# Two transformer blocks on one core: the two weight rings are moved 112 bytes past a multiple of 128

## The reference, cut to what matters

```python
def reference(x, ...):          # x: (1, 512, 1024) float32
    x = first_block(x, ...)     # rmsnorm, a 1024 -> 1536 projection, gated causal conv of 31 taps,
                                # layernorm, pools, 1024 -> 1024; then swiglu 1024 -> 2816 -> 1024
    return second_block(x, ...) # two layers: attention, layernorm,
                                # conv_ffn 1024 -> 2 x 2816 -> 1024, layernorm
def swiglu(x, w_gate, w_up, w_down):
    return (silu(x @ w_gate) * (x @ w_up)) @ w_down
```

## The kernel before, in words

| tensor | start within 128, before | after | distance of the moving tensor from its weights, before | after |
|---|---|---|---|---|
| XH, XL, yout, last_rows, raw | 0 | 0 | X from W: 0 | 16 |
| WH, WL | 0 | 112 | | |
| par, ones, identr, masks, work, small | 0 | 0 | | |
| HH, HL | 64 | 32 | H from W: 64 | 48 |
| PTH, PTL, OH, OL, OF, pmap, VX, QX and the rest of the attention | 64 | 96 | O from W: 64 | 112 |
| dg_h, dg_l | 64 | 64 | | |
| u_h, u_l, group 0 and group 1 | 64 + 4m and 124 + 4m | the same | u from dg: 4m and 60 + 4m | the same |

## Time and profile before

### The profile page before, as it was taken

How to read it: one execution, slowest core, us unless ns; L and a number is a source line. 1 busy time by engine, 2 the same in 40 slices (tenths; PEclk the granted TensorE clock), 3 DMA queues, 4 the chain that set the end, 5 groups by cost and what they waited for, 6 DMA issues and landing times.

```text
span 1818.9 us, 26859 instructions
## 1 busy us (share of the span) xinstructions
PE 1774.2 (98%) x8755; PEld 1477.6 (81%) x8755; DVE 765.2 (42%) x1382; ACT 795.8 (44%) x1674; POOL 1029.9 (57%) x926
## 2 busy tenths in 40 slices
PE   8999999999999999999999999999999999999997
PEld 6879888888887888788888888877777888888886
DVE  7963000001235556553333322487875533333224
ACT  5644323322245555464444422555565644444231
POOL 7856555555462333466666655555554666666551
PEclk9999999999999999999999999999999999999999
DMA  5312333323334454323333233333332233332332
GB/s 153 92 47 82 104 92 92 101 87 103 91 90 115 123 133 122 86 73 99 102 92 94 85 104 87 82 94 81 87 77 79 63 111 93 96 100 78 104 91 97
DMA packets 327253, 171.94 MB, mean 95 GB/s; under 512 B 43459, under 2 KB 316949, under 8 KB 327189
## 3 DMA queue, kind: packets, MB, share of 16 engines
q1 hardware_dynamic: 327172, 171.12, 33.8%
q10 hardware_dynamic: 16, 0.00, 0.0%
HBM read 152.15 MB, written 2.10 MB: 85 GB/s over the span
## 4 chain that ended last, share of the span: by engine, by line
PE 87%; DVE 5%; POOL 3%; ACT 2%; issue 1%; DMA 1%; SPq 0%; DVEq 0%; ACTq 0%; POOLq 0%
PE bank L982 24%; PE bank L984 24%; PE bank L983 24%; PE attended L982 2%; PE attended L983 2%; PE attended L984 2%; PE turned L1423 1%; POOL WL L741 1%; PE attended L1439 1%; PE bank L1055 1%; PE bank L1067 1%; POOL psums L804 1%; PE bank L1068 1%; DVE small L2453 0%; PE score L1406 0%
## 5 line engine op out<-in xcount | busy, mean ns | idle before, releaser
L741 POOL TENSOR_TENSOR WL<-raw,WH 128x512 fp32r<-128x512 f32 (+3 forms) x656 | 774.8, 1203 | 555.6 <-ACT WH L1604 553.1
L982 PE MATMUL bank<-XL,WH 128*128 128x512 f32 x1432 | 568.8, 397 | 3.7 <-DVE work L2576 1.2
L984 PE MATMUL bank<-XH,WL 128*128 128x512 f32 x1432 | 557.8, 390 | 0.0
L983 PE MATMUL bank<-XH,WH 128*128 128x512 f32 x1432 | 557.4, 389 | 0.0
L1604 ACT ACTIVATE WH<-raw 128x512 fp32r<-128x512 f32 (+3 forms) x656 | 338.5, 565 | 307.7 <-PE bank L984 190.9
L984 PEld LDWEIGHTS bank<-XH,WL 128*128 128x128 f32 x1432 | 269.7, 188 | 56.8
L982 PEld LDWEIGHTS bank<-XL,WH 128*128 128x128 f32 x1432 | 270.1, 189 | 55.6 <-DVE work L2576 1.5
L983 PEld LDWEIGHTS bank<-XH,WH 128*128 128x128 f32 x1432 | 270.4, 189 | 49.9
L982 PE MATMUL bank<-HL,WH 128*128 128x512 f32 (+1 forms) x528 | 200.6, 380 | 0.0
L983 PE MATMUL bank<-HH,WH 128*128 128x512 f32 (+1 forms) x528 | 200.3, 379 | 0.0
L984 PE MATMUL bank<-HH,WL 128*128 128x512 f32 (+1 forms) x528 | 200.3, 379 | 0.0
(11 more groups left out here) (366 smaller groups left out, 2532.0 us busy)
## 6 DMA issues: line engine op xcount, KB each, us to landing
raw<-in_ffn_w_in SPq DMA_DIRECT2D x88, 512.0 KB, 3.8
raw<-in_w_gate SPq DMA_DIRECT2D x22, 512.0 KB, 3.8
raw<-in_w_up SPq DMA_DIRECT2D x22, 512.0 KB, 3.9
raw<-in_ffn_w_out SPq DMA_DIRECT2D x28, 384.0 KB, 3.3
raw<-in_ffn_w_out SPq DMA_DIRECT2D x28, 320.0 KB, 3.2
raw<-in_a_w_in SPq DMA_DIRECT2D x16, 512.0 KB, 4.2
raw<-in_kv_w SPq DMA_DIRECT2D x32, 256.0 KB, 3.2
raw<-in_w_in SPq DMA_DIRECT2D x12, 512.0 KB, 3.8
```

What stands on the lines that cost most here:

```text
L741: pool.tensor_tensor(wl, x, wh, ALU.subtract).then_inc(w_lo, 1)
L982: pe.matmul(out_, wh, xl, start=start, stop=False)
L983: pe.matmul(out_, wh, xh, start=False, stop=False)
L984: return pe.matmul(out_, wl, xh, start=False, stop=stop)
```

## The change

The two rings get a room of their own and begin 16 bytes into it; three unused tensors (96, 96 and 32 bytes) move what follows. No instruction is added, removed or reordered; only addresses change. WH's room is 16384 + 128 bytes and WL's 16384 + 32, so that `par` and what follows it stay at multiples of 128.

```diff
-        WH = sb("WH", [P, SLOTS, DT, P], F32R)
-        WL = sb("WL", [P, SLOTS, DT, P], F32R)
+        sb("before_w", [P, 24])
+        WH = sb("WH", [P, SLOTS * DT * P + 32], F32R)[:, 4:4 + SLOTS * DT * P].rearrange("p (s k n) -> p s k n", s=SLOTS, k=DT)
+        WL = sb("WL", [P, SLOTS * DT * P + 8], F32R)[:, 4:4 + SLOTS * DT * P].rearrange("p (s k n) -> p s k n", s=SLOTS, k=DT)
...
         ffn = ExitStack()
+        sb("before_h", [P, 24], stack=ffn)
         HH = sb("HH", [P, FT, S], F32R, stack=ffn)
...
         att = ExitStack()
+        sb("before_o", [P, 8], stack=att)
         PTH = sb("PTH", [P, 2, QT * KEYS + S - P], F32R, stack=att)
```

## The result

Two runs of the changed kernel gave 1836.26 and 1841.02 us, median 1838.64, against 1817.22: a ratio of 1.0118, 95% interval 1.0087 to 1.0149. The change makes the kernel 21 us slower, where 22 us less had been forecast, and the time is outside the stated range. It lies near rival C (1844).

A forecast was written before the change was run, and what follows sets the result against it. It took PE's stream of matmuls, number times pitch, as the bound. Terms -8.9 - 1.0 - 11.9 + 1.7 - 2.5 + 0.8 = -21.8 us gave a median of 1795.4 us, range 1758 to 1824.

The forecast's parts named there:

- rival C: X's 512-column matmuls leave their best place, distance 0, and slow to 233.3 ns: +26.7 us, median 1844; chance 0.10.
- X from 0 to 16 bytes: X's matmuls against W each lose 2 ns: -8.9 us for 4440 of 512 columns, -1.0 us for 480 of 256.
- the forecast of 118: Pitch in ns forecast for 256-column matmuls at the new distances, from the convolution's taps, against 120 at distance 0.
- H from 64 to 48: H's matmuls against W: 512 columns fall to 224.7 ns, 8.6 less, -11.9 us; 256 columns cost +1.7 us.
- O stayed: O's matmuls against W, moved from 64 to 112: 8.9 ns less at 512 columns, -2.5 us; 256 columns cost +0.8 us.
- the work of ACT and POOL on WH and WL with odd starts: Writing and reading weight rings off multiples of 32 bytes: costed at nothing, up to +4 us over the run.
- B: The new distances have the small surplus, 512 columns at 220.4 ns: -52.1 us in all, median 1765; chance 0.27.
- D: No change: pitches come from something the change leaves alone, such as slice lengths or address bits above 128 bytes; 1817; chance 0.13.

The follow-up runs named there:

- all0: Against the kernel before: H and the attention's tensors moved 64 bytes on, so X, H and O are all at distance 0 from the weights; 1809.95 us, ratio 0.9968.
- w128: Against the kernel before: the rings and everything behind them moved by 128 bytes, X unmoved; 1842.03 us, ratio 1.0123.
- near: The change's distances (X 16, H 48, O 112 bytes) held within 512 and alike for WH and WL; 1821.53 us, ratio 1.0020 against the kernel before.
- w64: Against the kernel before: the rings alone moved by 64 bytes, putting X at distance 64 and H and O at 0 within 128; 1834.33 us, ratio 1.0104.
- h0odd: Against the kernel before: both rings moved 16 bytes on, H at exactly 0 within 512 from them, X at 496; one run, 1829.01 us.
- w16: Against the kernel before: the rings alone moved by 16 bytes, so they start at 16 within 32; one run, 1839.12 us.
- x16: Rings at 112 as in the change, H kept 64 bytes from them within 128, O's start as before; 1835.88 us, ratio 1.0115 against the kernel before.
- wl64: Against the kernel before: WL's ring alone moved 64 bytes on, X at 0 from WH and 192 from WL; one run, 1828.39 us.
- xl64: Against the kernel before: XL moved 64 bytes on from XH, with 128 bytes ahead of raw that also moved the rings by 128; one run, 1831.8 us.
- abs64: Against the kernel before: everything moved by 64 bytes, all distances kept and all absolute starts new; 1815.61 us, ratio 0.9993.
- w256: Against the kernel before: the rings and everything behind them moved by 256 bytes, X unmoved; 1817.50 us, ratio 1.0003.

## Why the prediction was wrong, point by point

**The bound was right.** A stream of matmuls whose pitch is set by placement, and no wait: PE's share stayed at 98%, and the time goes with the pitches of X and H: from 1810 us with both at 226.7 ns (all0) to 1842 with both at 233.3 (w128).

**The step that failed** is "X from 0 to 16 bytes", which took 2 ns off X's 4440 matmuls of 512 columns; they gained 6.1 ns each, +27.1 us in place of -8.9. Two things were wrong in it. First, it carried a difference from 256 columns to 512 "as distance 0 has the same surplus at both lengths". At 256 columns the forecast of 118 came out (O 117.7; H 119.9 in `down1`, 118.2 in `down2`, 118.7 over all its stages), and it told nothing of 512. At 512, distance 0 is the best of all that were measured, and at 256 it is among the worst. The two rows that showed 0 and 64 changing order between the lengths were warning enough. Second, the distance was taken within 128, as the table of starts did. Within 256 the change puts X 144 bytes from WH; near shows that at 16 bytes from both rings it would have been 228.4 ns and not 232.7. The same slip is in the rows that the step leaned on: by the sizes in the kernel u_h lies 128 bytes further from the diagonal weights than u_l within 256, so the tap of "distance 16" is one matmul at 16 and two at 144, and the three taps stand for no pure distance; that 118 came out of them is in part luck. And X against PTH is at 64 within 256, while H is at 192 from W, so those two slow readings were not of one distance. The counts were a little short too (4512 matmuls of X at 512 columns and 576 at 256, for 4440 and 480), which changes nothing.

**"H from 64 to 48"** was to give 8.6 ns and gave 1.1. H was at 192 within 256 and went to 176 and 48; at 48 from both rings (near) it is at 231.9 ns, so this distance doesn't act as 0 does. O stayed (233.8 for 233.6), where 8.9 ns less was forecast.

**Rightly costed at nothing:** the work of ACT and POOL on WH and WL with odd starts. One instruction took 566 and 1205 ns after, 565 and 1203 before, so there was nothing for PE's stream to cover.

**The rivals.** C had the mechanism, X leaving its best place, and its pitch (233.3 for 232.7); it was given 0.10. Its reason, that every place but 0 acts alike at 512 columns, holds for 32, 128, 160, 192 and 224 (233.3 to 234.3 ns) and fails at 16 and 64 (228.4 and 228.9). B's 220.4 ns was seen nowhere. D's forecast of no change is excluded by the result and by w64, which moves only the rings; but one of the causes that it named, bits of the address above 128 bytes, does count (w128). The rule of the Trainium skill that stood beside D ("TensorE: Matmul & The Clock Gate", "Step-by-step: what each phase is for", separate read ports for the moving operand and the weight load, so that the load takes no bandwidth from the running matmul) doesn't forecast this kernel's time: moving only the rings, with every instruction unchanged, cost 1.0% in w64. Whether the ports are shared after all no run here shows; the loss may come about in another way.

**Not settled.** What in the chip makes the pitch depend on the place of the tensors, and what picks one of two pitches where a placement shows both (h0odd, w16, x16). ACT and POOL write the rings while PE reads them; their accesses move with the rings too, and no run tells the effect of PE's own reads from that of such writes. wl64 points to a matmul and its own weights, but a stream that shows its delay one matmul late would look the same, and xl64 was spoiled by its layout. The next run would be a layout that moves XH against XL and holds both rings. A period over 256 is excluded only for distances 0 and 256.

## What to carry to other kernels

Where matmuls follow one another without waits, read their start-to-start pitch by tile from the timeline: two tiles of one shape with different pitches are worth a kernel that gives the slow one the other's distance to the weights (all0: 64 bytes of padding in two places, 0.3% faster). Take addresses from the built kernel and distances within at least 256 bytes, and keep starts at multiples of 32: the kernels that did so had one pitch for each placement at 512 columns. Read more than one stage, since a placement can show two pitches. Don't carry a placement effect from one matmul length to another.

## What the runs showed of the hardware that was not expected

- The pitch of 128x512 fp32r matmuls, each with its own weight load, ran from 226.7 to 234.3 ns when only addresses changed; for X it was 226.7 at a distance of 0 from the weights, 233.4 at 128 and 226.7 at 256, which fits a period of 256 bytes.
- At 256 columns the order is another: 113.5 to 113.8 ns at distance 192 in the stretches read here, where 512 columns are slow, and 119.9 ns at 0 (H in all0, 11.03 us for 92 matmuls), where 512 are quick.
- One placement can have two steady pitches in one execution. At 512 columns this was seen with starts at 16 within 32 only (X in h0odd, 226.7 ns in `gu0` and 233.3 in `gu1`). At 256 columns it comes with starts at multiples of 32 as well: in w256, O against W goes at 117.9 ns in `out1` (33 matmuls) and at 113.3 ns in `out2` (36):

```profile
773.87 0.28 PE L984 MATMUL bank<-OH,WH 128*128 128x256 f32 x1
...
777.76 0.28 PE L984 MATMUL bank<-OH,WH 128*128 128x256 f32 x1
...
1412.89 0.28 PE L984 MATMUL bank<-OH,WH 128*128 128x256 f32 x1
...
1416.97 0.28 PE L984 MATMUL bank<-OH,WH 128*128 128x256 f32 x1
```

- Starts at 16 within 32 cost H 3.3 to 4.4 ns at distance 0 (230.0 and 231.1 for 226.7, one execution).
- At 512 columns absolute starts made no difference when all moved together (abs64, ratio 0.9993).
